# Block sums of weights moved into the opening of a layer kernel, and the seven block products taken in another order

## What is computed

```python
def rms_norm(x, g):
    y = xf * lax.rsqrt(jnp.mean(xf * xf, axis=-1, keepdims=True) + EPS)
    return (y * g.astype(jnp.float32)).astype(x.dtype)
# h = x + W_out( sig(g_A) * Ret(RMSNorm(x)) + sig(g_B) * MLA(RMSNorm(x)) )
# h = h + SwiGLU(RMSNorm(h)); final RMSNorm
# D_MODEL 1024, RET_HEADS 4, MLA_HEADS 8, Q_LORA 512, KV_LORA 256, ROPE_DIM 64
```

## Time and profile before

| | us |
|---|---|
| median of 3 runs | 2094.2 (2093.69 to 2095.24) |
| the profiled execution | 2092.21 |
| its span in the profile | 2090.2 |
| TensorE busy | 1996.8 (96%) |
| VectorE busy | 1299.3 (62%) |
| ScalarE busy | 778.0 (37%) |
| GpSimd busy | 618.4 (30%) |

### The profile page before, as it was taken

How to read it: one execution, slowest core, us unless ns; L and a number is a source line. 1 busy time by engine, 2 the same in 40 slices (tenths; PEclk the granted TensorE clock), 3 DMA queues, 4 the chain that set the end, 5 groups by cost and what they waited for, 6 DMA issues and landing times.

```text
span 2090.2 us, 35246 instructions
## 1 busy us (share of the span) xinstructions
PE 1996.8 (96%) x14160; PEld 1926.2 (92%) x14160; DVE 1299.3 (62%) x2055; ACT 778.0 (37%) x1353; POOL 618.4 (30%) x581
## 2 busy tenths in 40 slices
PE   8989899998989899999999989999999999999997
PEld 8968788787989898999999989999999999999997
DVE  6567776865455555887767796655555555432257
ACT  5334444442233225555443335544344444210010
POOL 0134434422145341150000250664444444200000
PEclk9989999999999999999999999999999999999999
DMA  8335455464256447777785732122323232663412
GB/s 308 121 103 173 155 163 165 140 235 171 76 194 216 166 159 261 277 260 278 249 296 210 256 126 97 64 104 95 115 94 115 93 116 87 251 252 111 174 54 86
DMA packets 171425, 348.24 MB, mean 167 GB/s; under 512 B 14976, under 2 KB 81472, under 8 KB 163968
## 3 DMA queue, kind: packets, MB, share of 16 engines
q1 hardware_dynamic: 171264, 345.99, 47.7%
HBM read 234.22 MB, written 111.72 MB: 166 GB/s over the span
## 4 chain that ended last, share of the span: by engine, by line
PE 79%; DVE 10%; POOL 3%; DMA 3%; issue 3%; ACT 2%; SPq 1%; DVEq 0%; ACTq 0%; POOLq 0%
PE ps L1228 24%; PE ps L1230 24%; PE ps L1229 24%; DVE tmp L2217 1%; PE ps L1329 1%; PE ps L1421 1%; PE ps L1323 1%; DVE p_exp L2452 1%; DVE negmax L2444 1%; DVE qr L2210 1%; PE ps L1484 1%; PE ps L1480 1%; PE ps L1481 1%; DMA yd<-y_spill 1%; DVE pt_lo L2210 1%
## 5 line engine op out<-in xcount | busy, mean ns | idle before, releaser
L1228 PE MATMUL ps<-s_hi,t_hi 128*128 128x272 f32 x1344 | 389.1, 290 | 9.5 <-DVE s_lo L2210 9.5
L1230 PE MATMUL ps<-s_lo,t_hi 128*128 128x272 f32 x1344 | 390.8, 291 | 0.0
L1229 PE MATMUL ps<-s_hi,t_lo 128*128 128x272 f32 x1344 | 390.0, 290 | 0.0
L1228 PE MATMUL ps<-sx_hi,t_hi 128*128 128x272 f32 x1232 | 356.8, 290 | 2.2 <-ACT u L2066 2.2
L1229 PE MATMUL ps<-sx_hi,t_lo 128*128 128x272 f32 x1232 | 356.6, 289 | 0.0
L1228 PEld LDWEIGHTS ps<-s_hi,t_hi 128*128 128x128 f32 x1344 | 256.1, 191 | 10.4 <-DVE s_lo L2210 5.9
L1230 PE MATMUL ps<-sx_lo,t_hi 128*128 128x272 f32 x880 | 255.9, 291 | 0.0
L1230 PEld LDWEIGHTS ps<-s_lo,t_hi 128*128 128x128 f32 x1344 | 255.5, 190 | 0.0
L1229 PEld LDWEIGHTS ps<-s_hi,t_lo 128*128 128x128 f32 x1344 | 255.3, 190 | 0.0
L1228 PEld LDWEIGHTS ps<-sx_hi,t_hi 128*128 128x128 f32 x1232 | 234.6, 190 | 2.5 <-DVE t_lo L2210 2.4
L1229 PEld LDWEIGHTS ps<-sx_hi,t_lo 128*128 128x128 f32 x1232 | 234.2, 190 | 0.0
(11 more groups left out here) (285 smaller groups left out, 5061.4 us busy)
## 6 DMA issues: line engine op xcount, KB each, us to landing
job<-in_weights SPq DMA_DIRECT2D x96, 256.0 KB, 3.7
t_sums<-job SPq DMA_DIRECT2D x48, 512.0 KB, 3.6
t_row<-t_sums SPq DMA_DIRECT2D x48, 512.0 KB, 7.4
y_spill<-hg_r SPq DMA_DIRECT2D x44, 544.0 KB, 3.4
yd<-y_spill SPq DMA_DIRECT2D x22, 1088.0 KB, 5.6
s_raw<-s_x SPq DMA_DIRECT2D x21, 1088.0 KB, 5.6
t_row<-in_weights SPq DMA_DIRECT2D x36, 512.0 KB, 6.6
w_stage<-in_weights SPq DMA_DIRECT2D x35, 512.0 KB, 3.9
```

Source lines behind the costliest of these rows:

```text
L1228: nc.tensor.matmul(out, wh, xh, start=start, stop=False, skip_group_check=onto)
L1229: nc.tensor.matmul(out, wl, xh, start=False, stop=False, skip_group_check=onto)
L1230: return nc.tensor.matmul(out, wh, xl, start=False, stop=stop, skip_group_check=onto)
```

## The change

1. **Twelve jobs in the opening.** Jobs 0 to 11 go in four groups of three through six new tiles (`early_tile`). SyncE loads group 0 behind the cache's loads and the others between the spills and the items; groups 2 and 3 wait until the group that had their tiles has been stored (`early_out`). On GpSimd jobs 0 to 5 stand ahead of `power` for x, jobs 6 to 11 behind it and ahead of `shared_key(0)`. The tiles lie in space that is used again later, so ScalarE waits for the stores' landing in `latent(5)` and `shared_key`, VectorE ahead of `ckn`.
2. **The other 36 jobs thinner.** `job_turns` gives four jobs to seven turns of attention. The retention has none; `x_inv` is loaded ahead of it. The load of one item moves behind `xn_lo`'s in the last head.
3. **Octets.** Step 0 is A12·B21, copied by ScalarE to C11. Step 1, A11·B11, opens the bank and stays in it; VectorE adds it into C11. Steps 2 and 3 add on top and are copied out by ScalarE (`bank_copy`), step 4 is scaled by VectorE straight from the bank. So VectorE reads a bank 16 times per octet instead of 24, ScalarE 12 times instead of 4. In `MIX_OUT` VectorE adds each unit's bank once (`residual_added`), step 0's too, which had three additions. The places of C11 and C12 change over in the pieces' groups.

```diff
-OPENING_STEPS = (0, 2, 5)
+OPENING_STEPS = (0, 1, 5)
...
-ATTENTION_JOBS = 44
+OPENING_JOBS = 12
 def job_turns():
+    loads, stores = {}, {}
+    for i, job in enumerate(range(OPENING_JOBS, JOBS)):
+        first = 7 * (i // 4)
+        loads[divmod(first + (0, 1, 3, 5)[i % 4], 9)] = job
+        stores[divmod(first + (2, 4, 6, 7)[i % 4], 9)] = job
...
+            def early_load(group):
+                if group >= 2:
+                    sp.wait_ge(early_out[group % 2], 48)
+                elif group:
+                    sp.wait_ge(squared, 4)
+                for job in range(3 * group, 3 * group + 3):
+                    for tile in range(2):
+                        sp.dma_start(early_tile[job % 6][:, 2 * tile:2 * tile + 2, :].rearrange("p h (k c) -> p h k c", c=P),
+                                     job_source(job, tile)).then_inc(early_in[group % 2], 16)
...
+            early_load(0)
+            spill((0, 1))
+            items(4, 5)
+            spill((2, 3))
+            early_load(1)
+            early_store(0)
+            items(5, 6)
+            early_load(2)
+            spill((4, 5))
+            early_store(1)
+            items(6, 7)
+            early_load(3)
+            spill((6, 7))
+            early_store(2)
+            items(7, 8)
+            early_store(3)
...
-                        if at_turn == 0 and turn and late_job <= JOBS:
-                            job_store(late_job - 1)
-                        if at_turn == 1 and late_job < JOBS:
-                            job_load(late_job)
...
+            def residual_added(s, p):
+                c = (C11, C11, C21, C22, C12, C22, C21)[s]
+                dve.wait_ge(oct_done, UNITS * MIX_OUT + 4 * s + p + 1)
+                if s in (0, 2, 3, 4):
+                    wait_piece(dve, MIX_OUT, c, p)
+                at = quarters(piece(MIX_OUT, c, p)[:, :])
+                nc.vector.tensor_tensor(at, ps[:, 2 * p:2 * p + 2, 0:QUARTER], at, ALU.add).then_inc(o_read if s else o_copy, 1)
...
-            power(1, x_col)
+            for job in range(6):
+                job_sums(job)
+            power(1, x_col)
+            for job in range(6, OPENING_JOBS):
+                job_sums(job)
+            shared_key(0)
```

More of the change, by code:

```diff
@@ L57 @@
 JOBS = OCTETS * 4 * 2
+QUADRANT_OPERAND = {0: 1, 1: 0, 6: 6}
 C11, C12, C22, C21 = range(4)
@@ L91 @@
 G_END = G_A + 3 * N_A
-ATTENTION_JOBS = 44
+OPENING_JOBS = 12
 def job_place(job):
-    return (job % 2, job // 2) if job < ATTENTION_JOBS else (1, job - ATTENTION_JOBS // 2)
+    return job % 2, (job - OPENING_JOBS) // 2
 def job_turns():
[L108 to L118, removed]
+    loads, stores = {}, {}
[3 more added lines that the diff above has]
+        stores[divmod(first + (2, 4, 6, 7)[i % 4], 9)] = job
+    return loads, stores
 FIRST_JOB_ITEM, LAST_JOB_ITEM = 9, I_RET + 1
@@ L493, in build @@
         piece_in = [sem(f"piece_in{i}") for i in range(8)]
[L495 to L497 removed]
+        job_in, job_out, early_in, early_out = piece_in[0:2], piece_in[2:4], piece_in[4:6], piece_in[6:8]
+        JOBS_END, EARLY_END = 8 * (JOBS - OPENING_JOBS), 8 * OPENING_JOBS
+        PIECE_BASE = [2 * JOBS_END] * 2 + [JOBS_END] * 2 + [2 * EARLY_END] * 2 + [EARLY_END] * 2
         c_scaled = sem("c_scaled")
@@ L831, in _, with job_source @@
             sp.dma_start(ckn[:, :, TOK:KEYS], a["cache_ckv"]).then_inc(cache_ckv_in, 16)
[L832 to L837, removed]
+            def job_source(job, tile):
+                o, p, half = job // 8, job // 2 % 4, job % 2
+                first, step = OCTET_ITEMS[o]
+                return W[first + step * (p + 4 * tile)].rearrange("p (h k) c -> p h k c", h=2)[:, :, 2 * half:2 * half + 2, :]
@@ new lines, in job_target @@
+            def job_target(job):
+                o, p, half = job // 8, job // 2 % 4, job % 2
+                return t_sums[o, p, :, :, 2 * P * half:2 * P * (half + 1)]
+            def early_load(group):
[7 more added lines that the diff above has]
+                                     job_source(job, tile)).then_inc(early_in[group % 2], 16)
@@ new lines, in early_store, with spill @@
+            def early_store(group):
+                for job in range(3 * group, 3 * group + 3):
+                    sp.wait_ge(job_sum, 4 * job + 4)
+                    sp.dma_start(job_target(job), early_tile[job % 6][:, :, :]).then_inc(early_out[group % 2], 16)
+            def spill(tiles):
+                for t in tiles:
+                    wait_low(sp, t)
+                    sp.dma_start(xn_spill[:, 0, t, :], xa_hi[:, t, :].bitcast(F32)).then_inc(spill_out, 16)
+                    sp.dma_start(xn_spill[:, 1, t, :], xa_lo[:, t, :].bitcast(F32)).then_inc(spill_out, 16)
@@ L846, in items_ahead @@
             def items_ahead(what, h, kind, g):
-                if what == "M" and (kind, g) == ("K", 0):
+                if what == "M" and (kind, g) == ("K", 0) and h + 1 < MH:
                     items(mla_item(h, kind) + 2, mla_item(h, kind) + 3)
@@ L2625, in _ @@
                     late, m = divmod(g - 1, UNITS)
-                    if late in range(MIX_OUT) and m >= 16:
+                    if late in range(MIX_OUT) and m // 4 in (1, 5, 6):
                         result_scaled(late, RESULT_OF[m // 4], m % 4)
```

218 lines of the change are left out of this document (102 added, 116 removed).

## The result

| | before | after |
|---|---|---|
| median of the runs, us | 2093.69 (5 runs) | 2101.65 (2096.93 to 2104.32, 5 runs) |
| ratio after/before, 95% interval | | 1.0040 (1.0029 to 1.0051) |
| the profiled execution | 2092.21 | 2096.93 |
| its span | 2090.2 | 2095.0 |
| TensorE busy | 1996.8 | 1996.8 |

The kernel became 0.4% slower. The forecast was 2091.0 with a range up to 2101.0: the time lies outside, and on the other side of before. The profiled execution of the changed kernel is also the shortest of its five, so its 4.8 us more than before understate the change; the medians differ by 8.0.

What follows compares the result with a forecast made beforehand. TensorE, busy 96% of the span, was taken as the bound. Opening +14.9, attention −1.4, retention −13.3 and last octet −3.1 summed to −2.9, giving 2091.0 us; 8-in-10 range 2081 to 2101.

Steps and rivals of the forecast that it cites:

- the opening's ring: Opening: job groups' load, sum and store in turn; six loads put at six issues of 0.62 plus 3.7 us to landing.
- the five gated octets: Octets before the last: TensorE worked all 337 us from 884 to 1221, so less VectorE work gains nothing.
- Opening: +14.9 said: Opening: jobs ahead of TensorE's two row sums make it 14.9 us late, clock loss included.
- both chokes: Opening: TensorE's two row sums wait behind GpSimd's jobs, 5.7 us idle at the first, 4.2 more at the second.
- Rival 1: Opening: VectorE's reads stretch GpSimd's job operations, 0.99 for 0.73 us; second row sum 3 later, 2094 us; chance 0.15.
- rival 3: Opening: three landings SyncE waits for each come 1.5 us sooner, covering the second row sums' delay; 2085 us; chance 0.2.
- The bound of +18: Opening: upper bound of its loss in us, if GpSimd's job operations take longer there.
- My list of what would be wrong: Signs against the forecast: row sums on time, weights landing over 5 us after issue, TensorE waiting on ScalarE's bank copies.
- Attention: −1.4 said: Attention: 36 thinner jobs instead of 44 shorten TensorE's small waits by 1.4 us, with −4 and +2 as ends.
- Retention: −13.3 said: Retention: without job stores weights go out earlier, shrinking TensorE stalls of 6.1 and 6.8 us; −13.3, from −17 to −4.
- Rival 2: Retention: weights stay late because of prep loads, not the job's store; −4.2 instead of −13.3, 2100 us; chance 0.2.
- Last octet: −3.1 said: Start of the last octet: fewer VectorE additions ahead of two TensorE stalls, −3.1 us, from −1 to −5.

Runs made afterwards that it cites:

- octet_order_alone: The kernel before with only the octets' new order and ScalarE's bank copies, jobs as before: 2094.11 us, ratio 1.0004.
- store_behind_weights: The kernel before, with SyncE issuing a late job's store in retention one step later, behind the weights' loads (next load later too): 2081.80 us, ratio 0.9945.
- eight_jobs_sums_later: The changed kernel with eight opening jobs instead of twelve, 40 in attention, and GpSimd's gated sums in the second octet delayed: 2073.35 us, ratio 0.9910 against before.

## Why the prediction was wrong

Two steps failed: the time that six loads take in the opening's ring (3.7 us from the last issue to its landing said, 5.9 measured), and the five gated octets, put at nothing by the earlier trace rows (+3.0 measured in the second). Attention's +2.0 can't be judged.

**Opening: +14.9 said, +17.2 measured.** The mechanism was right, both chokes in their places. The first: `power` ended at 58.8 (58.1 said), row sums at 60.1 (58.9), clock 3.1 (3.0). The second: `early_load(2)` landed at 58.9 (57.3), `early_store(1)` at 68.3 (67.0), the fourth group's loads at 77.5 (73.5; by my own terms 67.0 and 6.8 make 73.8), row sums at 97.6 (93.8). What failed is the term of that ring, six loads. Their issues held: 3.3 us from the first to the last. But I took 3.7 from the last issue to its landing, the median of loads that go out in twos. In the third group it was 5.2. In the fourth the last was issued at 71.62 and took 5.9:

```profile
DMA to landing us min/median/max: 5.9/5.9/5.9
```

The stores ahead don't explain it, they had landed. The rate of the queue in the changed kernel, 66 to 80 us in 40 slices of 0.35:

```profile
GB/s 345 342 298 342 363 448 363 211 23 0 9 126 304 345 307 322 187 217 313 284 310 252 293 220 117 309 405 424 395 445 424 428 423 435 445 385 385 398 435 423
```

Behind SyncE's wait for the store's landing (to 68.36) the queue ran empty, from 69 to nearly 70 us. Then the six loads, issued 0.65 us apart, landed 0.95 to 1.8 apart, the last of them among the spills issued behind it. Until 74.7 the queue moved 117 to 345 GB/s, less than the 385 that I had taken for a full one. Why the loads land no faster is not shown. So the row sums came 3.8 later than said; the second stall's clock cost 1.4 for my 2.5, and 0.5 was won back behind it, which leaves the 2.3. Rival 1 wasn't it: jobs 9 to 11 took 9.5 us, 0.74 an operation. Nor did rival 3 come: no landing that SyncE waited for was 1.5 us sooner than I made it. The bound of +18 held for this execution; the other kernels with all twelve jobs there gave up to 20.2.

**Octets: nothing said, +3.0 measured in the second.** This step was wrong in kind. I read the earlier trace rows (337 of 337 us) as cover for any change to VectorE there and counted reads per octet: eight fewer. In step 1 it is more: before it scaled the bank straight from PSUM, 0.72 us; now it adds (0.72) and scales from SBUF (1.88), in the very units in which GpSimd's gated sums run. The low parts beside these sums took 2.45 there before as well (905.38), so they aren't the difference: from unit to unit VectorE went from 4.1 us to 5.9. A stage with no gap shows that less VectorE work buys nothing; it says nothing on where more of it falls. The trace of before had the prices at hand, in its timeline of VectorE: the scaling from SBUF beside GpSimd's sums at the end of the first octet, and a low part beside them in the last one, which takes 1.28 where GpSimd is quiet:

```profile
888.44 1.89 DVE L2593 TENSOR_TENSOR hg<-hg,x_inv 128x544 f32<-128x544 f32 x1
...
1235.28 2.41 DVE L2210 TENSOR_TENSOR s_lo<-hg,s_hi 128x1088 fp32r<-128x1088 f32 x1
```

My list of what would be wrong named ScalarE's copies; no wait of TensorE on them shows.

**Attention: −1.4 said, +2.0 measured.** Not to be judged. octet_order_alone and store_behind_weights have the jobs of before there and are 2.7 and 2.8 us longer over the same stretch than the profiled execution of before. A term under 3 us in this stage is below what one execution tells, and its bounds should have said so. One statement there was wrong, though: that `xn_lo` waits for TensorE's last use. In the changed kernel too it stood behind a job's load, which waited 10.5 us for the landing of that tile's last store (issued at 485.42, `xn_lo` at 487.39), and TensorE then stood for 8.0. eight_jobs_sums_later shows what that was worth.

**Retention: −13.3 said, −13.8 measured,** and −13.5 with the store's place alone. The two long waits fell by 4.3 and 4.4 us, and no granted clock of 0.50 follows either of them now, where it had been 0.50 for 10.2 us behind each. Rival 2 did not come true: the weights landed in 3.98 and 4.30. Whether the prep loads close ahead had a part in the 6.71 stays open, since they leave earlier in every kernel that mends it. Other executions gained 10.2 to 15.7, so that the fit within 0.5 is in part luck.

**Last octet: −3.1 said, −3.2 measured.**

**The sum** was −2.9 and became +4.8: 2.3 from the opening, 3.0 from the second octet, 3.4 from attention (of which some 2.7 lie in the execution of before), less 1.0 in the rest. The medians' further 3 us fit the opening's spread: the profiled execution had 17.2, the other three kernels with twelve jobs ahead of `shared_key` 19.1 to 20.2. That is an inference, since the longer executions have no trace. Slower had a chance of 0.22, nearly all of it rival 2's, and it came another way: by the opening and the second octet together. And the range ended at 2101 since I let one term go wrong at a time; only 0.02 was given to two at once.

## What to carry to other kernels

A store that waits for another engine, put in the one list of transfers ahead of a load that TensorE needs, cost here as much (13.5 us) as moving all jobs out of that stage won: first move the store. Work put into an idle engine's gap is bounded by the ring of load, work, store and landing and by every later user of its tiles, so count the rounds of the ring that fit (here two groups of three jobs and one of two did, and four groups of three did not in the orders that were run), and count a landing of several loads in a row from rows with as many. When a change takes operations from an engine, list its work unit by unit beside its neighbour's, and not per stage.

## What was not expected of the hardware

The last of six 256 KB loads in a row landed 5.2 and 5.9 us after its issue, with nothing but an item's weights and the other five on their way ahead of it and spills issued behind it, where the median of such loads in attention was 3.7. And two engines that read SBUF together stretched far more than the mean of the earlier trace rows suggests: VectorE 0.72 to 1.88, and one of GpSimd's job operations 1.78 instead of 0.74 beside VectorE's `w_lo` in the changed kernel's opening:

```profile
51.26 1.23 DVE L2247 TENSOR_TENSOR w_lo<-w_stage,w_hi 128x1024 fp32r<-128x1024 f32 x1 [0.40 <-ACT w_hi L1710]
```

```profile
51.31 1.78 POOL L2896 TENSOR_TENSOR early<-early 128x256 f32<-128x256 f32 x1
```
